# Attention's product with v moved one slab later, partly into the bank of the norms' totals

## What is computed

```python
# attention, per chunk of 64 tokens; the band is the chunk before and the chunk itself (128 keys)
scores = einsum("bnqhgd,bnkhd->bnhgqk", q, k_band) * HEAD_DIM ** -0.5
probs  = softmax(concat([scores, sink]))[..., :-1]
out    = einsum("bnhgqk,bnkhd->bnqhgd", probs, v_band)
y = concat([conv_group, out]) @ w_out
# MLP
val, gate = split(u @ w_up)
y = (val * silu(causal_dwconv(gate, w, b))) @ w_down
```

## Time and profile before

| | |
|---|---|
| median of 3 runs | 2107.39 us (2107.19 to 2108.32) |
| the profiled execution | 2107.35 us |
| its span in the profile | 2105.4 us |
| PE busy | 2070.4 us, 98% |
| DVE busy | 1189.1 us, 56% |
| ACT busy | 1025.9 us, 49% |
| POOL busy | 1406.3 us, 67% |

### The profile page before, as it was taken

The page is one execution under the profiler, slowest core; times in us unless marked ns, Lnnn a source line. Parts: engine busy times, 40 slices in busy tenths (PEclk is TensorE's granted clock), DMA queues, the critical chain, the costliest instruction groups (busy, mean ns, idle before and its releaser), DMA issues.

```text
span 2105.4 us, 27351 instructions
## 1 busy us (share of the span) xinstructions
PE 2070.4 (98%) x9619; PEld 1701.4 (81%) x9619; DVE 1189.1 (56%) x1945; ACT 1025.9 (49%) x1834; POOL 1406.3 (67%) x1773
## 2 busy tenths in 40 slices
PE   7999999999999999999999999999999999999997
PEld 6877778787888888888788888888778888888887
DVE  5888888575515554777632545687651454333235
ACT  3585356555516674374633656234552464433332
POOL 4987767856677887875567885564546776545554
PEclk9999999999999999999999999999999999999999
DMA  8654545533434354553233333332323232434332
GB/s 300 157 134 147 160 128 147 163 110 101 120 110 124 107 162 145 140 159 94 75 105 100 118 103 93 99 106 71 101 73 108 87 104 83 128 100 128 93 93 78
DMA packets 421508, 250.06 MB, mean 119 GB/s; under 512 B 48149, under 2 KB 393085, under 8 KB 421373
## 3 DMA queue, kind: packets, MB, share of 16 engines
q1 hardware_dynamic: 420506, 248.03, 40.1%
q10 hardware_dynamic: 867, 0.29, 0.1%
HBM read 242.71 MB, written 4.26 MB: 117 GB/s over the span
## 4 chain that ended last, share of the span: by engine, by line
PE 80%; POOL 8%; DVE 4%; ACT 4%; issue 3%; DMA 1%; SPq 0%; POOLq 0%; ACTq 0%; DVEq 0%
PE fg L862 25%; PE fg L864 25%; PE fg L863 25%; POOL w_lo L1884 4%; POOL ada_acc L1955 1%; PE bank_s L948 1%; DVE bank_c L1496 1%; ACT ada L1283 1%; DMA stage_in<-in_x_dram 1%; PE bank_l L874 1%; PE bank_t L970 1%; PE bank_l L885 1%; PE bank_t L957 0%; ACT w_hi L1127 0%; POOL ssum L1978 0%
## 5 line engine op out<-in xcount | busy, mean ns | idle before, releaser
L1884 POOL TENSOR_TENSOR w_lo<-raw,w_hi 128x256 fp32r<-128x256 f32 (+1 forms) x1425 | 1032.3, 756 | 626.7 <-ACT w_hi L1127 625.2
L862 PE MATMUL fg<-u_hi,w_hi 128*128 128x512 f32 x2112 | 838.6, 397 | 5.8 <-DVE u_lo L1476 2.1
L864 PE MATMUL fg<-u_hi,w_lo 128*128 128x512 f32 x2112 | 823.7, 390 | 0.0
L863 PE MATMUL fg<-u_lo,w_hi 128*128 128x512 f32 x2112 | 823.4, 390 | 0.0
L1127 ACT ACTIVATE w_hi<-raw 128x1024 fp32r<-128x1024 f32 (+2 forms) x387 | 375.6, 970 | 386.5 <-PE fg L864 282.9
L862 PEld LDWEIGHTS fg<-u_hi,w_hi 128*128 128x128 f32 x2112 | 397.0, 188 | 103.9 <-issue 16.2
L864 PEld LDWEIGHTS fg<-u_hi,w_lo 128*128 128x128 f32 x2112 | 397.0, 188 | 84.6
L863 PEld LDWEIGHTS fg<-u_lo,w_hi 128*128 128x128 f32 x2112 | 397.4, 188 | 81.8 <-issue 2.6
L1496 DVE SCALAR_TENSOR_TENSOR bank_c<-glu,par,bank_c 128x512 f32<-128x512 f32 x448 | 306.1, 747 | 0.1
L1838 DVE SCALAR_TENSOR_TENSOR x<-fg,mod,x 128x512 f32<-128x512 f32 (+1 forms) x168 | 121.6, 724 | 320.0 <-PE fg L864 319.8
L864 PE MATMUL fg<-h_hi,w_lo 128*128 128x512 f32 (+1 forms) x704 | 269.8, 383 | 0.0
(11 more groups left out here) (264 smaller groups left out, 1846.2 us busy)
## 6 DMA issues: line engine op xcount, KB each, us to landing
raw<-in_w_up_dram SPq DMA_DIRECT2D x176, 512.0 KB, 3.8
ada<-in_w_ada_ffn_dram SPq DMA_DIRECT2D x48, 512.0 KB, 4.5
raw<-in_w_down_dram SPq DMA_DIRECT2D x64, 384.0 KB, 3.4
raw<-in_w_in_dram SPq DMA_DIRECT2D x40, 512.0 KB, 3.9
raw<-in_w_down_dram SPq DMA_DIRECT2D x64, 320.0 KB, 3.1
ada<-in_w_ada_mix_dram SPq DMA_DIRECT2D x32, 512.0 KB, 4.3
raw<-in_w_in_dram SPq DMA_DIRECT2D x32, 256.0 KB, 3.8
raw<-in_w_out_dram SPq DMA_DIRECT2D x32, 256.0 KB, 2.9
```

What stands on the lines that cost most here:

```text
L862: pe.matmul(out, hi[:, k, :], rhi, start=k == order[0], stop=False)
L863: pe.matmul(out, hi[:, k, :], rlo, start=False, stop=False)
L864: ins = pe.matmul(out, lo[:, k, :], rhi, start=False, stop=k == order[-1])
L1884: ins = pool.tensor_tensor(lo_of(n)[:, ks, :], raw[n % NRAW][:, ks, :], hi_of(n)[:, ks, :].bitcast(F32), ALU.subtract)
```

## The change

The step `pv` of mixers 1 to 3 is planned on the `uv` slab, between `sc` and `mx`/`tr`, and not on the `ug` slab ahead of it. Where that `uv` slab lies outside every layer norm (`in_norm` is false), the product goes into `bank_l` and stays there. Where it lies inside one, the step is taken out and put at the end of the list of the `ug` slab ahead, and the product goes into `bank_t` as before. Mixer 0 is as before.

By the rule of the diff, `bank_l` gets chunks 0 to 6 of mixer 1 (slabs 57, 59, 61, 63, 65, 75 and 77), 0 to 3 of mixer 2 (161, 163, 173, 175) and 0 to 2 of mixer 3 (259, 261, 271): 14 in all. The other ten stay on their `ug` slab, behind its other steps. The planner's room follows the step: a `ug` slab of these has 27 instead of 22 left and takes three taps instead of two, and its `uv` slab 18 instead of 23 (11 instead of 16 with an `as`), two instead of three (one instead of two). For mixer 2 the last tap so moves from slab 177 to slab 176, and the whole norm (`cm`, `cc`, `cv`, `cq`, `cd`, `cr` and what follows) one slab ahead: `cm` from 178 to 177, `cv` with `cq` and `cd` from 181 to 180, `cr` from 183 to 182. For mixers 1 and 3 the norm stays on its slabs.

```diff
@@ def attention(mi, n):
             if SLABS[n][0] == "ug":
-                chunk_step(n, mi, ("pr", p - 1), ("pv", p - 2))
-                chunk_step(n + 1, mi, ("sc", p), ("mx", p), ("tr", p - 1))
+                chunk_step(n, mi, ("pr", p - 1))
+                chunk_step(n + 1, mi, ("sc", p), ("pv", p - 2), ("mx", p), ("tr", p - 1))
@@ behind plan()
+def in_norm(n):
+
+    return any(min(slots((k + m, i))) <= n <= max(slots((k + e, i))) for k, m, e, i in NORM_SPANS)
+
+
+PV_BANK = {(0, _i): "f2" for _i in range(NCH)}
+for _mi in range(1, len(MIXERS)):
+    for _i, _n in enumerate(slots(("pv", _mi))):
+        PV_BANK[_mi, _i] = "t" if in_norm(_n) else "l"
+        if in_norm(_n):
+            STEPS[_n].remove(("pv", _mi, _i))
+            at(_n - 1, "pv", _mi, _i)
 SUM_BANK = {}
 for _c in range(CHUNKS_BEFORE, 4 * NCHUNK):
     _n, = slots(("as", _c))
-    _norm = any(min(slots((k + m, i))) <= _n <= max(slots((k + e, i))) for k, m, e, i in NORM_SPANS)
-    SUM_BANK[_c] = "t" if _norm else "l"
+    SUM_BANK[_c] = "t" if in_norm(_n) else "l"
@@ def pv_bank(mi, i):
-            return bank_t if mi else fg[2]
+            return {"f2": fg[2], "t": bank_t, "l": bank_l}[PV_BANK[mi, i]]
@@ def weigh_v(mi, i):
-                if mi:
-                    take("t", alo, n + 1)
-                else:
-                    take("f2", alo, n + 1)
+                take(PV_BANK[mi, i], alo, n + 1)
```

## The result

The changed kernel takes 2132.85 us (median of 4 runs, 2131.05 to 2134.61), against 2107.29 (4 runs, 2106.84 to 2108.32): a ratio of 1.0122 [1.011, 1.0135]. The prediction said 2119.9 and at most 2125. Slower was right. The size was not: +25.6 us in place of +12.5.

What follows compares the result with a forecast made beforehand. PE, 98% busy, was taken to bound the kernel through its matmuls and waits. 8.9 + 0.4 + 3.7 + 1.2 - 1.9 - 0.7 = +11.6, plus 0.9 for the clock, on 2107.35 gave 2119.9 us; range 2111.5 to 2125.

Steps and rivals of the forecast that it cites:

- The waits for the fold: Slabs 61, 65, 163: PE's product waits until DVE has read the fold in `bank_l`; 2.7 + 3.1 + 3.1 = 8.9 us.
- ACT's cycle: ACT's chain over a pair of slabs with `ad` in both: 14.15 us, against 13.43 before and 13.0 that PE needs.
- Two small ones of 0.2: Small DVE instructions with the maxima, counted in the 2.05 us placed on DVE ahead of ACT's exponentials.
- the wait for the scaled probabilities: Slab 59: the transposes wait for the scaled probabilities, by which some 0.4 us of ACT's lateness comes back.
- 2.3 - 0.4: ACT put 2.3 us back by slabs 56 to 59, less 0.4 at slab 59; taken as 1.8 late at slab 61.
- the 0.8 for the pair ahead of slabs 65 and 163: A pair with `ad` puts ACT 0.8 us back, raising each fold wait there from 2.3 to 3.1.
- The clock: PE's clock falling to half rate at the new waits: priced at one fall, 0.9 us, half of the 1.8 seen earlier.
- the clock falls at every long wait: Rival: a fall of 1.8 us at each of four waits (three folds and slab 181), 2126 us; chance 0.14.
- the old wait of 1.9: PE's product with v waiting for the copy of the transposed probabilities, five times; forecast to go, 1.9 us saved.
- `a_lo` behind the root: Slabs 180 and 276: `a_lo` behind the reciprocal root delays the next slab's transposes, 2.3 and 1.4 us, together 3.7.
- Joining: `pv` sharing a slab boundary with `sc` and `tr` costs 0.76 instead of 0.81: 0.05 saved 14 times, 0.7 us.
- POOL's total: Mixer 2's norm one slab ahead: PE waits 1.2 us for POOL's sum at slab 177 (bounds 0.8 and 1.6).

Runs made afterwards that it cites:

- narrow_adds: Changed kernel with GpSimd's accumulating modulation adds covering 32 columns in place of 512, the other columns left out of the sum; 2126.24 us, ratio 1.0087.
- norm_place: Changed kernel with the products that stay in `bank_t` put back behind `pr` instead of at the end of the `ug` slab's list; 2129.36 us, ratio 1.0106.
- the remedied one: Changed kernel with the planner's room as before, maxima ahead of `a_lo` on DVE, and products at folds and norms at their old place; 2103.93 us, ratio 0.9988.
- maxima_first: Changed kernel with only DVE's order changed, the maxima ahead of `a_lo` and, in `uv` slabs without a fold, of `h_lo`; 2118.06 us, ratio 1.0055.

## Why the prediction came out as it did

*The waits for the fold* were the right step with a mis-sized term: 12.3 instead of 8.9 (3.60, 4.45 and 4.25 instead of 2.7, 3.1 and 3.1). The part of it that failed is ACT's cycle. "Two small ones of 0.2" behind the maxima is wrong where POOL adds at the same time; one of them takes 1.0 to 1.2. 14.15 + 0.8 = 14.95 is the measured 14.9. Two pairs make ACT 1.6 later than I had it: 0.8 of that came out in slab 59 (the wait for the scaled probabilities was 1.2, not 0.4), and 0.9 in slab 61 (3.6, not 2.7). narrow_adds confirms both numbers: 0.34 there, and 2.78. Two slips of the text are too small to matter: 2.3 - 0.4 is 1.9 and not 1.8, and the 0.8 for the pair ahead of slabs 65 and 163 has no working beside it, where 14.15 - 13.0 is 1.15.

*The clock* was the largest error and the step that failed most: 5.5 (by the rows 6.3) instead of 0.9. I had taken one fall at half of its price, because the waits have dense work ahead of them. That work protects nothing here: three of the four long waits had their fall. The rival "the clock falls at every long wait" was near the price, 1.8 each where the rows give 1.6 to 2.5, and had all but one of the places. The Trainium skill ("TensorE: Matmul & The Clock Gate", section "HAM oscillation — how this bites in real kernels") describes a kernel in which the half rate comes back at every gap in the matmul stream. The trace agrees in three of four places, and not in slab 61, where 3.60 us went by without a fall. That section's gaps are waits of some 3 to 5 us, so my sentence that by its rule each of the waits forecast here, 2.3 to 3.1 us, would bring a fall went further than it does.

*The copies of the probabilities.* I took the old wait of 1.9 off and put none in its place. But the ten products that stay on their `ug` slab need the copy as early as before, and ACT is late there too:

```profile
1027.49 0.65 PE L980 MATMUL bank_t<-probs_t,v 128*64 128x256 f32 x4 [1.33 <-ACT probs_t L1273]
```

With slab 272 (0.79) this is 2.1 us that I didn't foresee. In slab 279 `a_lo` came 0.8 late behind another step, unforeseen as well.

*What was right.* `a_lo` behind the root: 2.33 in slab 181 and 1.41 in slab 277, forecast 2.3 and 1.4. Joining: the boundary with all three steps is 2.10 in place of 0.81 + 1.37, so 0.08 saved each time, 1.1 in all, forecast 0.7. POOL's total: 0.4, forecast 1.2; PE comes to it later by the 1.33 of slab 176. No wait for a slab's bank or for weights was added.

The sum with the measured terms, the clock by the rows: 12.3 + 1.2 + (2.33 + 1.41 + 0.8 =) 4.5 + 2.1 + 0.4 - 1.9 - 1.1 + 6.3 = 23.8, against 23.7 between the two profiled spans. That it fits so closely is in part luck: the last fold ahead of mixer 1's attention starts at 374.21 after and at 375.39 before, so the changed stretch lost 24.9, and 1.1 of it is in none of these terms. The last 1.9 up to the 25.6 between the medians is that the profiled execution after was the fastest of its four. The range failed by its upper end: the high ends of the waits (+14.7) and four falls were each in the text, and were not added to each other. The +14.7 with three falls of 1.8 give 2127.5, still 5.4 short of the time. The unforeseen waits (2.1 and 0.8) are 2.9 of that, and the waits for the fold, 2.3 above their high bound of 10, are the most of the rest.

What stays open is why the clock held through 3.60 us in slab 61 and fell at the 2.33 us of slab 181. The slab doesn't decide it: in norm_place the clock fell at slab 61, behind 3.61.

## What to carry to other kernels

When a step is given another buffer, write down for each new neighbour in that buffer which engine reads it and when that engine's own queue gets there: the bank that looked free cost 12.3 us by a reader that stood behind a whole slab of vector work. On an in-order engine, put the instruction that another engine's long chain waits for (here the maxima) ahead of the one whose reader has a slab of time; that swap was worth 14.8 us in the changed kernel and 5.6 in the remedied one. And price a new wait of 2 to 5 us of TensorE with the clock's fall on top; here that was 1.6 to 2.5 us each in three cases of four.

## What the runs showed of the hardware that I had not expected

A small DVE instruction can last as long as GpSimd's instruction beside it. L1652 and L1655 read two tensors of 128x4 in SBUF and take 0.16 us with no such add beside them, but 0.98 at 398.92 and 1.18 at 443.32, each to the end of GpSimd's 128x512 add within 0.03 us; with adds of 32 columns (0.3 us each) the one at 398.56 took 0.16 again. L1650, ahead of them, reads PSUM and keeps its 0.68. The Trainium skill ("SBUF — State Buffer", section "SBUF: two separate sides") has this as a port pair that VectorE, when it reads two SBUF inputs, and GpSimd hold in turn, each for a whole instruction; these rows agree.

The clock's fall is not set by the length of the wait alone, nor by its place. In the changed kernel 2.33, 4.25 and 4.45 us brought it and 3.60 did not; in norm_place 3.61 at the same slab brought it, and so did 1.87 behind POOL's sum. In maxima_first it fell behind 2.39 us (slab 163) and held through 2.36 (slab 65).
